# A two-layer diffusion step with experts: five PSUM banks for turning x, and four smaller edits

## The chip, the cores and the metric

One core of a Trainium2 chip runs the whole program: TensorE (matrix multiplies), VectorE (DVE), ScalarE (ACT), GpSimd (POOL) and SyncE (SP, which only issues DMAs here), with a banked accumulator memory (PSUM, eight banks of 512 fp32 columns per partition) and on-chip memory (SBUF). The metric is the device time of one execution in microseconds, as the median of three runs.

## The reference, cut to what matters

Two layers act on 384 rows of 1024 values: 128 context rows and 256 latent rows, handled as three tiles of 128 rows. With `norm` an RMS norm and `sh`, `sc`, `gt` vectors computed from a conditioning vector, one layer is

```
h = rms_norm(x, norm_g[l, 0]) * (1 + sc_m) + sh_m
y = token_mixer(h)                                # 8 attention heads, gated MLP heads, a short convolution
x = x + gt_m * rms_norm(y, norm_g[l, 1])
h = rms_norm(x, norm_g[l, 2]) * (1 + sc_f) + sh_f
f = swiglu(h) if l == 0 else moe_swiglu(h)        # (silu(h @ Wg) * (h @ Wu)) @ Wd, width 2816
x = x + gt_f * rms_norm(f, norm_g[l, 3])
```

`moe_swiglu` takes logits `h @ w_router` (1024 x 8), picks the two best experts of each row, and adds their SwiGLU outputs weighted by a softmax over the two logits. All weights are fp32 and are read once from memory.

## The kernel before, in words

Every product of full precision is three matmuls in the fast `fp32r` type: a value is split in a rounded part (`whi`, `xhi`, `hhi`) and a rest (`wlo`, `xlo`, `hlo`), and `three` (L1285) issues hi x hi, hi x lo, lo x hi. Weights come as 1 MB chunks in the order of one list (`stream`, L64) through a ring of six buffers `raw`: SP may load chunk n when TensorE has finished chunk n-6 (L433). ACT rounds each chunk to `whi` (`split`, L622 to L628), which waits for TensorE to be done with the chunk three before, and DVE makes `wlo` (L890). `upto(n)` on either engine means that all chunks up to n are split.

Each engine has one hand-written instruction order, joined to the others by semaphores. Around each of the four sub-layers the order is the following, with s = 0 to 3 counting (layer 0 mixer, layer 0 FFN, layer 1 mixer, layer 1 router).

The end of a sub-layer is `residual`. TensorE finishes y of tiles 0, 1 and 2 in PSUM banks 0 to 5. For each tile ACT squares and sums y (`rms`, L638) and takes the square root (L640); DVE takes the reciprocal (L901), multiplies (L973) and adds to x (L975). Shortly before, TensorE spreads the gate row over the partitions and ACT copies it (`gates`, L688). ACT's functions lie in tables that are loaded when a function outside the current table comes up; Exp, Silu, Gelu and Sqrt need different ones, Copy, Square and Identity none of their own. 

The next sub-layer begins with `norm`. ACT sums the squares of the new x (L638, L640), and DVE scales each tile of x into `f` (`scaled`, L948). TensorE turns x: for each of the eight k-tiles of 128 columns, three transposes (`turn_x`, L1354) bring the k-tile of the three row tiles into one PSUM bank. For s >= 1 the banks are 6 and 7 in turn (`turn_banks`, L358), and the turn of k-tile kt waits until the one of kt-2 has been read (L1380). ACT scales and shifts it into `hf` (L662 for the context rows, L663 for the latent rows), and for s < 3 DVE makes `xhi` (L955) and `xlo` (L957). The mixer's first products wait k-tile by k-tile (L1526). The dense FFN of layer 0 waits for all eight (L1752), then `gate_up` (L1649) runs over b = 0 to 10 column blocks, two chunks each; block b writes banks 0, 2, 4 or 1, 3, 5.

For s = 3, the router, TensorE puts after each turn the logits of the k-tile two before (`logits`, L1344: 24 small fp32 matmuls), and ACT alone writes `hf`. DVE then picks the experts (L1218 on), TensorE turns `hf` back to rows (L1760), counts rows per expert (L1767, L1771), and POOL scatters the rows (L583) and gathers those of each expert (L592). The experts follow, 33 chunks each, with as many row tiles as they were given (1, 1.5, 2 or 3).

At the very end POOL gathers for each row tile t the two expert outputs, `yg[:, 0, t]` and `yg[:, 1, t]` (L612), both on semaphore `s_yg[t]`. DVE multiplies the first by its gate (L1274) and adds the second times its gate (L1275), for all three tiles; then comes `residual(3, 1, 1)`, and ACT stores x (L879).

## Time and profile before

| what | value |
|---|---|
| three runs | 1779.31, 1783.63 and 1784.79 us, median 1783.63 |
| the profiled execution | 1779.33 us, of which its span is 1777.6 |
| mean granted TensorE clock | 0.963 of full |
| busy: TensorE matmul, DVE, ACT, POOL | 93%, 61%, 52%, 10% |
| DMA | 422 MB, mean 237 GB/s |

Times of the trace count from the span's start. Four stretches lie between sub-layers and are named in what follows: the first from 233 to 263 us (mixer to dense FFN), the second from 538 to 573 us (dense FFN to the second mixer), the third from 761 to 826 us (second mixer through the router to the experts), and the last from 1742 us on. A row of the timeline gives the start and duration in us, engine, line, operation and operands; `xN` merges N alike, and brackets give the idle time before it and what ended it. PEclk is the granted share of TensorE's full clock of 2.4 GHz; it has two levels, 1.0 and 0.5.

### The profile page before, as it was taken

The page shows a single profiled execution, that of the slowest core. Times are in us where ns is not written, and L with a number is a line of the kernel's source. Part 1 is how long each engine was busy: PE and PEld are TensorE (multiplying, and loading weights), DVE is VectorE, ACT ScalarE, POOL GpSimd, SP SyncE. Part 2 cuts the span into 40 slices and gives each one's busy share as a digit, 9 for nine tenths or more (in the row PEclk, how much of TensorE's full clock was granted, in tenths as well). Part 3 has the DMA queues.
Part 4 walks back from the last instruction along what each step waited for, and adds up shares of the span by engine and source line. Part 5 has one row for each costly group of instructions (what it writes and reads, how often), then busy time and mean ns, then how long its engine had stood idle before and what let it go on. Part 6 is the DMA issues. An engine that isn't in the chain of part 4 may idle for free.

```text
span 1777.6 us, 21764 instructions
## 1 busy us (share of the span) xinstructions
PE 1650.7 (93%) x8658; PEld 1293.1 (73%) x8658; DVE 1089.5 (61%) x1204; ACT 926.5 (52%) x1137; POOL 170.9 (10%) x178
## 2 busy tenths in 40 slices
PE   5799979999998899975999999999999999999993
PEld 2567758888776567754887877878787777787782
DVE  2336563333235326644998989898988866657653
ACT  1425452323225325453777777777777755455541
POOL 2400000000003000002021020303030100010001
PEclk9999979999998999986999999999999999999996
DMA  9973223333465872315999999999999976676643
GB/s 334 342 263 143 90 72 110 127 119 119 166 234 153 294 261 84 99 63 169 358 369 350 378 350 376 349 381 350 370 358 358 357 217 209 213 228 211 202 155 120
DMA packets 295809, 422.11 MB, mean 237 GB/s; under 512 B 21792, under 2 KB 226592, under 8 KB 295584
## 3 DMA queue, kind: packets, MB, share of 16 engines
q1 hardware_dynamic: 281504, 394.85, 65.7%
q0 software_dynamic: 13056, 23.11, 4.3%
q10 hardware_dynamic: 1136, 2.64, 0.4%
q8 instruction: 73, 1.20, 0.3%
q14 instruction: 40, 0.33, 0.1%
HBM read 418.56 MB, written 19.27 MB: 246 GB/s over the span
## 4 chain that ended last, share of the span: by engine, by line
PE 85%; DMA 4%; DVE 4%; ACT 2%; issue 2%; SPq 1%; POOL 1%; POOLq 0%; DVEq 0%; ACTq 0%
PE ps L1287 23%; PE ps L1289 22%; PE ps L1288 22%; PE ps L1293 3%; PE ps L1294 3%; DMA raw<-in_w_in_dram 2%; PE ps L1643 2%; PE ps L1329 1%; PE ps L1721 1%; SPq L436 1%; PE ps L1354 1%; DMA raw<-in_w_ada_dram 1%; PE ps L1477 1%; PE ps L1461 1%; PE ps L1311 1%
## 5 line engine op out<-in xcount | busy, mean ns | idle before, releaser
L890 DVE TENSOR_TENSOR wlo<-raw,whi 128x2048 fp32r<-128x2048 f32 x327 | 747.3, 2291 | 327.4 <-ACT whi L628 324.7
L628 ACT ACTIVATE whi<-raw 128x2048 fp32r<-128x2048 f32 x327 | 625.9, 1917 | 341.4 <-DMA raw<-in_w_in_dram 108.7
L1287 PE MATMUL ps<-whi,xhi 128*128 128x512 f32 (+1 forms) x1352 | 546.3, 404 | 18.2 <-DVE wlo L890 11.0
L1289 PE MATMUL ps<-whi,xlo 128*128 128x512 f32 (+1 forms) x1352 | 528.3, 391 | 0.0
L1288 PE MATMUL ps<-wlo,xhi 128*128 128x512 f32 (+1 forms) x1352 | 527.7, 390 | 0.0
L1287 PEld LDWEIGHTS ps<-whi,xhi 128*128 128x128 f32 x1352 | 258.2, 191 | 86.8 <-DVE wlo L890 25.2
L1289 PEld LDWEIGHTS ps<-whi,xlo 128*128 128x128 f32 x1352 | 257.6, 191 | 54.2
L1288 PEld LDWEIGHTS ps<-wlo,xhi 128*128 128x128 f32 x1352 | 258.5, 191 | 47.7 <-issue 0.5
L1287 PE MATMUL ps<-whi,hhi 128*128 128x512 f32 x484 | 196.3, 405 | 0.4 <-DVE pg L1007 0.4
L1289 PE MATMUL ps<-whi,hlo 128*128 128x512 f32 x484 | 189.5, 391 | 0.0
L1288 PE MATMUL ps<-wlo,hhi 128*128 128x512 f32 x484 | 189.1, 391 | 0.0
L1289 PEld LDWEIGHTS ps<-whi,hlo 128*128 128x128 f32 x484 | 90.9, 188 | 19.6
L1287 PEld LDWEIGHTS ps<-whi,hhi 128*128 128x128 f32 x484 | 91.0, 188 | 19.0 <-DVE pg L1007 1.2
L1288 PEld LDWEIGHTS ps<-wlo,hhi 128*128 128x128 f32 x484 | 91.2, 188 | 17.0 <-issue 0.2
L592 POOL DMA_INDIRECT hx<-h_rows,lidx x24 | 49.7, 2073 | 522.1 <-PE ps L1721 430.8
L718 ACT ACTIVATE pg<-ps 128x256 f32<-128x256 f32 x121 | 43.5, 380 | 97.2 <-PE ps L1643 88.2
L1005 DVE TENSOR_TENSOR pg<-pg,ps 128x256 f32<-128x256 f32 x121 | 48.6, 417 | 71.0 <-ACT pg L718 60.3
L731 ACT ACTIVATE xhi<-ps 128x384 fp32r<-128x384 f32 x64 | 31.5, 492 | 85.4 <-PE ps L1721 84.8
L605 POOL DMA_INDIRECT y_rows<-f,lidx x24 | 44.0, 1832 | 326.0 <-ACT f L757 319.3
L1329 PE MATMUL ps<-raw,cS 128*32 128x512 f32 x384 | 53.5, 675 | 21.9 <-DMA raw<-in_w_ada_dram 21.9
L1293 PE MATMUL ps<-whi,xhi 128*128 128x512 f32 x176 | 68.6, 390 | 1.8 <-DVE xhi L1026 1.8
L1294 PE MATMUL ps<-wlo,xhi 128*128 128x512 f32 x176 | 68.6, 390 | 0.0
(219 smaller groups left out, 1287.8 us busy)
## 6 DMA issues: line engine op xcount, KB each, us to landing
raw<-in_w_moe_gu_dram SPq DMA_DIRECT2D x352, 512.0 KB, 6.5
raw<-in_w_moe_d_dram SPq DMA_DIRECT2D x176, 512.0 KB, 6.3
raw<-in_w_ada_dram SPq DMA_DIRECT2D x96, 512.0 KB, 10.0
raw<-in_w_in_dram SPq DMA_DIRECT2D x44, 512.0 KB, 7.5
raw<-in_w_ffn_gu_dram SPq DMA_DIRECT2D x44, 512.0 KB, 4.6
raw<-in_w_ffn_d_dram SPq DMA_DIRECT2D x22, 512.0 KB, 6.9
raw<-in_w_out_dram SPq DMA_DIRECT2D x16, 512.0 KB, 4.4
bias<-rpb_rows POOLq DMA_DIRECT2D x32, 96.0 KB, 4.3
```

The source lines that it names most:

```text
L592: pool.indirect_dma_start(out=hx[:, i, :], out_offset=None, in_=h_rows[:, :], in_offset=bass.IndirectOffsetOnAxis(ap=lidx[:, e, i:i + 1], ...
L605: pool.indirect_dma_start(out=y_rows[:, :], out_offset=bass.IndirectOffsetOnAxis(ap=lidx[:, e, i:i + 1], axis=0), in_=f[:, i, :], in_offse ...
L628: act.activation(whi[m % SPL][:, :], raw[n % RING][:, :], ACT.Copy).then_inc(s_hi, 1)
L718: ins = act.activation(pg[:, t, :], ps[:, 2 * t + b % 2, 0:256], ACT.Silu)
L890: dve.tensor_tensor(wlo[n % RING][:, :], raw[n % RING][:, :], whi[NTH[n] % SPL][:, :].bitcast(F32), ALU.subtract).then_inc(s_lo, 1)
L1005: ins = dve.tensor_tensor(pg[:, t, :], pg[:, t, :], ps[:, 2 * t + b % 2, 256:512], ALU.mult)
L1287: pe.matmul(out, a_hi, w_hi, start=start, stop=False)
L1288: pe.matmul(out, a_hi, w_lo, start=False, stop=False)
L1289: return pe.matmul(out, a_lo, w_hi, start=False, stop=stop)
L1293: pe.matmul(out, a, w_hi, start=start, stop=False)
L1294: return pe.matmul(out, a, w_lo, start=False, stop=stop)
L1329: ins = pe.matmul(ps[32 * k:32 * k + 32, bank, :], cS[:, 4 * h + k, :], w[:, k, :], start=(h == 0), stop=(h == 1))
```

## The change

1. `turn_banks`: five banks in turn in place of two for s >= 1, and turn kt waits for the reader of kt-5 in place of kt-2.
2. For the dense FFN, the wait for all of `xlo` before `dense()` goes; in block 0, row tile 0, TensorE waits for each k-tile's `xlo` ahead of its products. It still issues the eight turns first.
3. The router: ACT writes `hf` for the even k-tiles, DVE for the odd ones (semaphore `s_hfd`), and all logits come after all turns.
4. `fetch_roots`: a square root of one column on ACT before each `gates`, and once after the experts.
5. The last combination: ACT multiplies the first choice by its gate (`first_choice`), DVE adds the second, and DVE's residual of tile t-1 comes between the combinations of t and t+1. Each gather has its own semaphore.

```diff
         def turn_banks(s):
-            return [6, 7] * (KT // 2) if s else list(range(KT))
+            if s == 0:
+                return list(range(KT))
+            free = [1, 3, 5, 6, 7] if s == 1 else [3, 4, 5, 6, 7]
+            return (free + free)[0:KT]
+
+        def rows_out(eng, kt):
+            eng.wait_ge(s_hfd if kt % 2 else s_hf, KT * 3 + kt // 2 + 1 if kt % 2 == 0 else kt // 2 + 1)
...
-                for kt in range(KT):
+                for kt in range(0, KT, 2 if s == 3 else 1):
                     act.wait_ge(s_tr, KT * s + kt + 1)
...
                 for t in range(NT):
                     if s == 3:
+                        if t + 1 < NT:
+                            first_choice(t + 1)
                         act.wait_ge(s_yc, t + 1)
...
+            def fetch_roots():
+                act.activation(root[:, :], eps[:, :], ACT.Sqrt)
+
+            def first_choice(t):
+                act.wait_ge(s_yg[0][t], 16)
+                act.activation(yg[:, 0, t, :], yg[:, 0, t, :], ACT.Copy, scale=gates_of[:, 0, t:t + 1]
+                               ).then_inc(s_ya, 1)
...
                 upto(n - 1)
+                fetch_roots()
                 gates(2 * l)
...
                     upto(PLACE["ffn", 0, N_FFN - 1])
+                    fetch_roots()
                     gates(1)
...
             by_tiles(act, "act", T, expert)
+            fetch_roots()
+            first_choice(0)
             residual(3, 1, 1)
...
                 if s:
                     scaled(s, l, half)
-                for kt in range(KT if s < 3 else 0):
+                if s == 3:
+                    dve.wait_ge(s_modc, 2 * l + half + 1)
+                    for kt in range(1, KT, 2):
+                        dve.wait_ge(s_tr, KT * s + kt + 1)
+                        sh, sc = modc[:, 2 * half, kt, :], modc[:, 2 * half + 1, kt, :]
+                        for g, a, b in ((0, 0, P), (1, P, 3 * P)):
+                            ins = dve.tensor_scalar(hf[:, kt, a:b], ps[:, turn_banks(s)[kt], a:b], sc[:, g:g + 1],
+                                                    sh[:, g:g + 1], ALU.mult, ALU.add)
+                        ins.then_inc(s_hfd, 1)
+                    return
+                for kt in range(KT):
...
             for t in range(NT):
-                dve.wait_ge(s_yg[t], 32)
-                chain(dve.tensor_scalar(yg[:, 0, t, :], yg[:, 0, t, :], gates[:, 0, t:t + 1], None, ALU.mult))
+                dve.wait_ge(s_yg[1][t], 16)
+                dve.wait_ge(s_ya, t + 1)
                 dve.scalar_tensor_tensor(out=yg[:, 0, t, :], in0=yg[:, 1, t, :], scalar=gates[:, 1, t:t + 1],
                                          in1=yg[:, 0, t, :], op0=ALU.mult, op1=ALU.add).then_inc(s_yc, 1)
-            residual(3, 1, 1)
+                if t:
+                    residual(3, 1, 1, [t - 1])
+            residual(3, 1, 1, [NT - 1])
...
             def norm(s):
                 for kt in range(KT):
-                    if kt == 1 and s % 2 == 0:
+                    if kt == 1 and s == 2:
                         pe.wait_ge(s_modc, s + 1)
-                    if kt >= 2:
-                        pe.wait_ge(s_hf, KT * s + kt - 1)
+                    if kt >= 5:
+                        if s == 3:
+                            rows_out(pe, kt - 5)
+                        else:
+                            pe.wait_ge(s_hf, KT * s + kt - 4)
                     turn_x(s, kt)
-                    if s == 3 and kt >= 2:
-                        if kt == 2:
-                            pe.wait_ge(s_wr, 16)
-                        logits(kt - 2)
                 if s == 3:
-                    for kt in (KT - 2, KT - 1):
-                        pe.wait_ge(s_hf, KT * s + kt + 1)
+                    pe.wait_ge(s_wr, 16)
+                    for kt in range(KT):
+                        rows_out(pe, kt)
                         logits(kt)
...
                             for kk in range(4):
                                 kt = 4 * h + kk
+                                if ready is not None and b == 0 and t == 0:
+                                    ready(kt)
...
-                gate_up(NT, 0, n0)
+                def ready(kt):
+                    pe.wait_ge(s_xlo, KT + kt + 1)
+
+                gate_up(NT, 0, n0, ready=ready)
...
                 norm(2 * l + 1)
                 if l == 0:
-                    pe.wait_ge(s_xlo, KT * 2)
                     dense()
```

## Rows read from the trace of the kernel before

**Rows 1.** The page, chain that ended last: shares of the span by engine
```profile
PE 85%; DMA 4%; DVE 4%; ACT 2%; issue 2%; SPq 1%; POOL 1%; POOLq 0%; DVEq 0%; ACTq 0%
```

**Rows 2.** Windows (us, each engine's busy time, PEclk, DMA share, GB/s): an expert
```profile
931.00:1030.00 99.00, 99.00 (x448) 78.85 (x447) 87.97 (x75) 74.95 (x76) 14.73 (x8) 1.00 1.06 363
```

**Rows 3.** Timeline, first stretch: ACT and DVE around the first square root
```profile
234.45 0.60 ACT L688 ACTIVATE f<-ps 128x512 f32<-128x512 f32 x1 [6.68 <-PE ps L1624]
...
239.56 2.29 DVE L890 TENSOR_TENSOR wlo<-raw,whi 128x2048 fp32r<-128x2048 f32 x1 [9.46 <-ACT whi L628]
...
241.08 1.28 ACT L640 ACT_TABLE_LOAD   x1
...
242.71 0.16 DVE L901 RECIPROCAL rs<-rs 128x1 f32<-128x1 f32 x1 [0.85 <-ACT rs L640]
```

**Rows 4.** Timelines of PE, ACT and DVE, first stretch: the turns of x
```profile
253.39 1.12 PE L1354 MATMUL ps<-ident,f 128*128 128x128 f32 x4 [0.39 <-DVE f L948]
...
263.20 0.80 PE L1287 MATMUL ps<-whi,xhi 128*128 128x512 f32 x1 [2.74 <-DVE xlo L957]
...
253.97 0.46 ACT L662 ACTIVATE hf<-ps,modc 128x128 f32<-128x128 f32 x1 [1.70 <-PE ps L1354]
...
254.77 0.46 ACT L662 ACTIVATE hf<-ps,modc 128x128 f32<-128x128 f32 x1
...
254.91 0.36 DVE L955 CAST xhi<-hf 128x384 fp32r<-128x384 f32 x1 [1.58 <-ACT hf L663]
...
255.78 0.35 DVE L955 CAST xhi<-hf 128x384 fp32r<-128x384 f32 x1
...
260.63 1.05 DVE L955 CAST xhi<-hf 128x384 fp32r<-128x384 f32 x1
```

**Rows 5.** Timelines of DVE and PE, second stretch
```profile
552.33 2.29 DVE L890 TENSOR_TENSOR wlo<-raw,whi 128x2048 fp32r<-128x2048 f32 x1 [5.49 <-ACT whi L628]
555.80 0.16 DVE L901 RECIPROCAL rs<-rs 128x1 f32<-128x1 f32 x1 [1.17 <-ACT rs L640]
...
566.48 1.11 PE L1354 MATMUL ps<-ident,f 128*128 128x128 f32 x4 [0.39 <-DVE f L948]
...
573.19 0.78 PE L1287 MATMUL ps<-whi,xhi 128*128 128x512 f32 x1
...
575.90 0.43 PE L1287 MATMUL ps<-whi,xhi 128*128 128x512 f32 x1
```

**Rows 6.** Timelines of PE and DVE, third stretch: turns and logits
```profile
781.18 1.12 PE L1354 MATMUL ps<-ident,f 128*128 128x128 f32 x4 [0.38 <-DVE f L948]
...
783.55 0.51 PE L1344 MATMUL ps<-wr,hf 128*32 128x8 f32 x24
...
789.92 0.83 PE L1344 MATMUL ps<-wr,hf 128*32 128x8 f32 x48
...
791.57 0.18 DVE L1218 COPY lg<-ps 128x24 f32<-128x24 f32 x1 [10.45 <-PE ps L1344]
```

**Rows 7.** Instructions of tile f: DVE's scaling of 256 columns from PSUM
```profile
L1083 DVE TENSOR_SCALAR f<-ps x16: 414/414/416, 159.1 to 722.0; 128x256 f32<-128x256 f32 x16
```

**Rows 8.** Windows of 2 us: the clock's rise, first and third stretch
```profile
268.00:270.00 2.00, 2.00 (x9) 1.61 (x8) 0.00 (x0) 0.00 (x0) 0.00 (x0) 0.81 0.00 0
...
794.00:796.00 2.00, 1.85 (x14) 1.40 (x13) 0.53 (x5) 1.44 (x4) 0.00 (x0) 0.89 0.00 0
```

**Rows 9.** Timeline of the last stretch, DVE
```profile
1758.37 0.75 DVE L1274 TENSOR_SCALAR yg<-yg,gates 128x1024 f32<-128x1024 f32 x1 [13.36 <-DMA yg<-y_rows,idx]
...
1761.83 0.75 DVE L1274 TENSOR_SCALAR yg<-yg,gates 128x1024 f32<-128x1024 f32 x1 [1.39 <-DMA yg<-y_rows,idx]
...
1764.49 0.75 DVE L1274 TENSOR_SCALAR yg<-yg,gates 128x1024 f32<-128x1024 f32 x1 [0.58 <-DMA yg<-y_rows,idx]
...
1773.29 1.23 DVE L975 TENSOR_TENSOR x<-x,yg 128x1024 f32<-128x1024 f32 x1
```

**Rows 10.** Instructions of tile yg: the six gathers from issue to landing
```profile
DMA to landing us min/median/max: 4.5/5.8/6.3
```

More of the change, by code:

```diff
@@ L958, in norm, with residual @@
                                       ).then_inc(s_xlo, 1)
-            def residual(s, l, half):
+            def residual(s, l, half, tiles=range(NT)):
                 r = 5 * l + 2 + 2 * half
-                for t in range(NT):
+                for t in tiles:
                     g = min(t, 1)
@@ L1647, in turn, with gate_up @@
                     ins.then_inc(s_ht, 1)
[L1649 removed]
+            def gate_up(T, k, n0, free=None, half=0, ready=None):
                 for b in range(GU_B):
```

9 lines of the change are left out of this document (6 added, 3 removed).

## The prediction

> **What bounds the kernel.** I read the page first. Part 4 puts 85% of the chain that ended last on TensorE [rows 1], so the kernel is a long stream of matmuls, and time can only be won where TensorE stands still or runs slow. The waits of TensorE and the merged chain then say where: at the four stretches between sub-layers. I read those instruction by instruction in the timelines of each engine, and the clock in windows of 2 us. The experts I read in one window each: TensorE is busy all the time at full clock, and the DMA engines are as full, at 363 GB/s [rows 2]. So nothing is to be won inside the experts. What starts them earlier counts in full only if the weight stream starts earlier too. It does: SP loads a chunk when TensorE has finished the one six before, so with the ring full the stream waits for TensorE. Before the experts the DMA share is 0.00 [rows 8].
>
> **The square root table (edit 4).** In the first stretch ACT ends its squares and loads a table for 1.28 us; only then come the root and DVE's reciprocal at 242.71 [rows 3]. The early load falls in the 6.68 us in which ACT waits for the gates' matmul [rows 3], so it costs nothing; without that cover it would cost its 1.28 us in front of the gates, which is no more than it saves. What is late next is DVE: its `wlo` ends at 239.56 + 2.29 = 241.85, so the reciprocal comes at about 241.8, 0.9 us earlier and not 1.28. From there DVE works in one chain through three tiles and three scalings, so x reaches TensorE 0.9 us earlier. In the second stretch `wlo` ends at 554.62 and the reciprocal stood at 555.80 [rows 5]: 1.15 us. The third has the first's pattern: 0.9 us. In the last the load is off the path already.
>
> The Trainium skill, "ScalarE: Activation LUTs", section "What ACT_TABLE_LOAD costs", counts about 2.66 us for a switch, of which some 1.38 is a drain. Here the root follows the load directly and the load is 1.28, so the measurement decides. By the page each of the three loads would hide twice as much, but DVE's `wlo` would cap the gain at the values above all the same, or at most 1.4 us more each if the drain lay on this path.
>
> **First stretch: five banks and the FFN by k-tile (edits 1, 2).** The last transposes of k-tile 0 begin at 253.39. Four take 1.12 us of which one's own length is 0.47, so they start 0.215 us apart, 0.65 us per k-tile [rows 4]. ACT needs 254.77 - 253.97 = 0.80 us for a k-tile, DVE 255.78 - 254.91 = 0.87 us [rows 4]. With two banks the three engines took turns, and TensorE then waited 2.74 us for the last `xlo`, until 263.20.
>
> After: with the 0.9 us, k-tile 0's last transpose starts at 252.5. Counting it, 22 transposes remain, 22 x 0.215 = 4.7 us, if the bank is free each time. K-tile 5 is due at 252.5 + 13 x 0.215 = 255.3 and needs ACT's k-tile 0 (about 254.0), k-tile 7 is due at 256.6 and needs ACT's k-tile 2 (about 255.6). So no wait: the turns end at about 257.3. The FFN's chunks 0 and 1 are split before the residual. Its first product needs `xlo` of k-tile 0, ready at 255.78 - 0.9 = 254.9, and k-tile 3 is ready at about 257.6, or 258.3 if the slow cast of 1.05 us [rows 4] falls on it. At the low clock a k-tile's three matmuls take 1.3 us, so TensorE asks for k-tile 3 at 261.2. K-tiles 4 to 7, ready by 262, are asked for after 12 k-tile products, past 270. The eight new waits therefore cost nothing, and the products start at 257.3 and not at 263.2: 5.9 us, the table's 0.9 within it. The bounds: 2 us if the turns run only at ACT's pace, or if xlo starves the products; 6.5 us if nothing waits.
>
> **The clock.** In this stretch the granted clock is at 0.5 until about 268.8 (0.81 over 268 to 270 is 0.76 us at the low level) [rows 8], 5.6 us after the first product. In the second it comes back at about 575.9, 2.7 us after the first product at 573.19: before it six matmuls take 2.71 us, 0.45 each, against about 0.22 in an expert [rows 5, 2]. In the second there was no gap between turns and products, and so it will be in both now. If the first goes from 5.6 to 2.7 us at half speed it gains 1.4; if the second goes the other way it loses 1.4. I take 0.6 for the first, near the middle, and 0 for the second. For both together the ends are -1.4 and +2.8.
>
> **Second stretch (edit 1).** K-tile 0's last transpose moves from 566.48 to 565.33, and 22 x 0.215 later, at 570.1, the first product can start, in place of 573.19 [rows 5]. It already waited k-tile by k-tile; `xlo` 0 is ready at about 567.8, k-tile 3 at about 570.8 while TensorE asks for it at 574. Gain 3.1 us, the table's 1.15 within it. POOL's DMAs fall in the same time and DVE's casts are slower in places; at the low end 1.5 us.
>
> **Third stretch (edits 1, 3).** TensorE was nearly the bound of the router: from 781.18 to the logits' copy at 791.57, with a turn and a logits group in 1.27 us [rows 6]. The last two groups ran together in 0.83 us with 0.20 for one's length, or 0.32 a group; in alternation one cost 0.44. After: start 780.3, turns until 785.0 as above, then 0.3 us to switch, 8 x 0.32 = 2.6 us and 0.2 for the last, so the copy comes at 788.2: 3.4 us, of which 0.9 the table's. DVE's new pair costs 0.41 for 256 columns [rows 7] and by that row some 0.28 for 128, 0.6 to 0.7 in all; it does four, ACT four at 0.80. Both keep up with 1.3 us of turns per pair. K-tile 7 is written by 786.1, and its logits are asked for at 787.5. If the logits keep 0.44 a group the gain is 2.4. Behind it the clock stays at 0.5 until 794.2 [rows 8], inside the turning back of hf. If it still rises at that hour, what then stands in front at the low clock costs about 0.5 us more; if it doesn't rise before the counting matmuls, about 3. I take 3.0 us, bounds 0.4 and 3.6. Scatters, gathers and experts hang on this chain and shift whole.
>
> **Last stretch (edit 5).** DVE's third combination waits for its gather (0.58 us idle), the end of x is 1773.29 + 1.23 = 1774.52 [rows 9]. From the second pair's landing at 1761.8 DVE now has two combinations of 1.31 and three residuals of 2.65 (reciprocal, 1.28, 1.23 and the gaps): 10.6 us, to 1772.4. ACT must keep up. The gathers land 4.5 to 6.3 us after issue [rows 10], and tile 1's first choice about halfway between 1758.3 and 1761.8 [rows 9], so ACT has it scaled at 1761.2, does tile 0's squares and root until 1762.7, before DVE asks at 1763.1; then scales tile 2 until 1764.2, and tile 1's root is ready at 1765.7 while DVE asks at 1766.9. The new wait in front of `rms` on ACT has tile 0's squares behind it and costs nothing here. If tile 1's first choice lands only with its second, DVE is 1.1 us later. Gain 2.1, bounds 0.8 and 2.3.
>
> **Sum.** 5.9 + 0.6 + 3.1 + 3.0 + 2.1 = 14.7 us. Against the profiled execution, 1779.33, that is 1764.6. The median before is 1783.63, 4.3 above it, for which the trace has no reason, so I set the sum against the median: 1768.9.
>
> **The rivals.**
> - The gain is partly eaten: turns go at ACT's pace or the first products starve, and the router's matmuls stay in the low clock. Then 2 + 1.5 + 0.4 + 2.1 and little from the clock, with some of these at their better end: about 8 us, 1775.6. For it: at 0.65 against 0.80 us per k-tile ACT is the slower engine, and DVE slower still. Against it: five banks' slack covers eight k-tiles.
> - Edit 4 does not do what it says, the tables being loaded again at the roots: 0.9 + 1.15 + 0.9 less, 11.8 us, 1771.8. Against it: copies after a root in this trace bring no load.
> - The weight stream takes it back: the experts' DMA is full at 363 GB/s [rows 2]. If it, and not TensorE's start, set the end, only the last stretch would count: 1781.5. Against it: a share of 0.00 before the experts [rows 8].
> - Slower than before: the clock. Without the idle gap TensorE goes from turns to products at 0.5, and if it is not granted full speed for long afterwards, each us at the low level costs half a us. From 29 us more at 0.5 the gain is gone, and 40 us more in both blocks together gives 1789. For it: the level does fall in every stretch. Against it: it rose within 2.7 to 5.6 us of the first product in the two stretches.
>
> **Chances.** The forecast, with its own range 1764 to 1774, 0.60; table again 0.05; partly eaten 0.22; stream 0.08; clock 0.03; the remaining 0.02 is more than the sum. What this measurement can tell from no change is 0.3%, 5.4 us. From the cases: faster 0.88, same 0.09, slower 0.03. The range is 1762 to 1777, with the spread of the three runs, up to 4 us below and 1 above the median, in it.
>
> **What will show it.** No ACT_TABLE_LOAD between the first squares and their root in the three stretches; reciprocals directly behind `wlo`. The first FFN product 4 to 5 us after the last scaling of x, straight behind the 24th transpose. The lg copy about 8 us after k-tile 0's last transpose. DVE without a gap from the second landing to the end. It would be wrong if the first products show waits for xlo, if an expert takes longer than before, or if the low clock lasts over 10 us into a sub-layer.

## The result, and the profile after

| what | before | after |
|---|---|---|
| median, and the runs behind it | 1781.99 us, 4 runs (1779.31 to 1784.79) | 1760.11 us, 4 runs (1759.11 to 1761.90) |
| ratio of the two | | 0.9878, 95% interval 0.9859 to 0.9898 |
| profiled execution, its span | 1779.33, 1777.6 | 1759.84, 1758.1 |
| mean granted clock | 0.963 | 0.969 |

The kernel became faster by 1.2%: 21.9 us by the medians, 19.5 us between the two profiled executions. The forecast was 1768.9 with a range of 1762 to 1777. The direction was right, the size was 8.8 us short, and the time lies below the range.

To see where the 19.5 us came from, I cut both spans at the same eleven instructions. A stage here runs from the instruction in its first column to the next one's.

```
stage, from ... to ...                                      before   after    diff
start, to the gates' matmuls of the first stretch           233.40  234.03   +0.63
first stretch, to the first FFN product                      29.80   23.66   -6.14
dense FFN, to the gates' matmuls of the second stretch      275.19  273.16   -2.03
second stretch, to the mixer's first product                 34.80   31.54   -3.26
second mixer, to the gates' matmuls of the third            188.00  186.58   -1.42
third stretch, to DVE's copy of the logits                   30.38   24.74   -5.64
picking, scatter and gather, to the first gathered turn      26.01   25.37   -0.64
to the experts' first product                                 9.02    9.02    0
experts, to the last gates' matmul                          919.52  921.08   +1.56
last stretch, to the end of x                                28.40   25.85   -2.55
to the end of the span                                        3.08    3.07    0
```

The first, fifth and ninth lines carry the spread from one execution to the next. Over the sixteen profiled executions behind this document the start takes 230.2 to 236.6 us. The experts take 919.3 to 922.1 (925.8 in one) and the second mixer 185.7 to 190.9. Where the code of the stage is the same as in the kernel after, the first stretch takes 23.0 to 23.7 us, the FFN 272.6 to 273.2, the second stretch 30.6 to 31.6, and the last stretch 25.7 to 26.6. The third took 24.74 us where the low clock (below) lasted 6.8 us, and 26.14 in e7, where it lasted 10.2.

The page of the kernel after: part 1 and the chain that ended last by engine, to be set beside [rows 1]. TensorE's share of the chain fell from 85% to 81%.

```profile
PE 1637.8 (93%) x8658; PEld 1288.4 (73%) x8658; DVE 1090.2 (62%) x1209; ACT 924.9 (53%) x1136; POOL 172.6 (10%) x178
...
PE 81%; DMA 7%; DVE 6%; ACT 2%; issue 2%; SPq 1%; POOL 1%; POOLq 0%; DVEq 0%; ACTq 0%
```

Timelines of ACT, DVE and PE of the kernel after, first stretch, which answer to [rows 3, 4]:

```profile
241.49 0.19 ACT L649 ACTIVATION_READ_ACCUMULATOR hf<-ps 128x1 f32 x1
241.71 0.29 ACT L651 ACTIVATE rs<-ss,eps 128x1 f32<-128x1 f32 x1
...
240.19 2.29 DVE L917 TENSOR_TENSOR wlo<-raw,whi 128x2048 fp32r<-128x2048 f32 x1 [9.47 <-ACT whi L639]
242.40 0.16 DVE L928 RECIPROCAL rs<-rs 128x1 f32<-128x1 f32 x1
...
253.08 4.96 PE L1393 MATMUL ps<-ident,f 128*128 128x128 f32 x22 [0.39 <-DVE f L975]
257.69 0.78 PE L1326 MATMUL ps<-whi,xhi 128*128 128x512 f32 x1
258.69 0.40 PE L1328 MATMUL ps<-whi,xlo 128*128 128x512 f32 x1
...
258.06 1.21 DVE L992 CAST xhi<-hf 128x384 fp32r<-128x384 f32 x1
```

No table load stands between the squares and the root, and the reciprocal follows `wlo` at once. All 22 remaining transposes form one row of 4.96 us, where four stood in a row before. The product comes directly behind them, without a bracket and so without a wait. The durations of the products show the clock, which came back to full speed at 258.7: the first takes 0.78 us, the third 0.40.

The second stretch of the kernel after, timelines of DVE and PE (compare [rows 5]):

```profile
544.77 2.29 DVE L917 TENSOR_TENSOR wlo<-raw,whi 128x2048 fp32r<-128x2048 f32 x1 [5.47 <-ACT whi L639]
546.98 0.15 DVE L928 RECIPROCAL rs<-rs 128x1 f32<-128x1 f32 x1
...
557.78 4.89 PE L1393 MATMUL ps<-ident,f 128*128 128x128 f32 x22 [0.39 <-DVE f L975]
562.39 0.52 PE L1326 MATMUL ps<-whi,xhi 128*128 128x512 f32 x1
```

And the third (compare [rows 6]). The turns and the logits are now two rows, and the second turning follows:

```profile
768.02 3.91 PE L1393 MATMUL ps<-ident,f 128*128 128x128 f32 x22 [0.39 <-DVE f L975]
771.86 1.79 PE L1383 MATMUL ps<-wr,hf 128*32 128x8 f32 x192
773.58 1.09 PE L1803 MATMUL ps<-ident,hf 128*128 128x128 f32 x8
...
769.24 0.86 DVE L986 TENSOR_SCALAR hf<-ps,modc 128x128 f32<-128x128 f32 x2 [1.28 <-PE ps L1393]
773.71 0.18 DVE L1255 COPY lg<-ps 128x24 f32<-128x24 f32 x1 [0.76 <-PE ps L1383]
```

The same 22 transposes take 3.91 us here and about 4.9 in the first two stretches. The reason stands in the windows of 2 us (columns as in [rows 2]: PEclk is third from the right). Of the kernel after:

```profile
258.00:260.00 2.00, 2.00 (x9) 1.59 (x8) 1.97 (x4) 2.00 (x6) 1.60 (x3) 0.83 0.00 0
562.00:564.00 2.00, 2.00 (x11) 1.74 (x10) 1.94 (x4) 2.00 (x7) 2.00 (x4) 0.88 0.56 146
770.00:772.00 2.00, 2.00 (x30) 1.83 (x33) 1.65 (x5) 1.74 (x5) 0.00 (x0) 0.83 0.00 0
```

A PEclk of 0.83 over 2 us is 0.68 us at the low level (1.2 GHz in place of 2.4) and the rest at full. Narrower windows give the edges. The low periods about the three stretches were 20.5, 13.6 and 17.1 us long before and are 10.2, 6.8 and 6.8 us after. Before, the clock came back 5.6 us behind the first FFN product, 2.8 behind the mixer's, and 2.8 behind the logits' copy [rows 8]. After, it comes back 1.0 us behind the first FFN product, at the mixer's first product, and at 770.7, two thirds through the router's turns.

The last stretch, DVE of the kernel after (compare [rows 9]), with ACT's new multiply:

```profile
1742.49 1.15 ACT L704 ACTIVATE yg<-yg,gates 128x1024 f32<-128x1024 f32 x1 [2.06 <-DMA yg<-y_rows,idx]
...
1744.59 1.28 DVE L1312 SCALAR_TENSOR_TENSOR yg<-yg,gates 128x1024 f32<-128x1024 f32 x1 [2.06 <-DMA yg<-y_rows,idx]
...
1753.80 1.23 DVE L1012 TENSOR_TENSOR x<-x,yg 128x1024 f32<-128x1024 f32 x1
```

From 1744.59, when the second pair of rows has landed, to 1755.03 DVE never waits.

### The profile page after: what moved, and what is told of

Its sections match the earlier page's. It is cut to its first block, busy times and chain, and to the rows that moved or that the text cites. A ratio compares the mean times of both kernels' runs of the same rounds, so it can differ in the third digit from the quotient of the medians.

```text
span 1758.1 us, 21774 instructions
## 1 busy us (share of the span) xinstructions
PE 1637.8 (93%) x8658; PEld 1288.4 (73%) x8658; DVE 1090.2 (62%) x1209; ACT 924.9 (53%) x1136; POOL 172.6 (10%) x178
## 4 chain that ended last, share of the span: by engine, by line
PE 81%; DMA 7%; DVE 6%; ACT 2%; issue 2%; SPq 1%; POOL 1%; POOLq 0%; DVEq 0%; ACTq 0%
PE ps L1326 22%; PE ps L1328 21%; PE ps L1327 21%; DMA raw<-in_w_in_dram 3%; PE ps L1332 3%; PE ps L1333 3%; DMA raw<-in_w_moe_gu_dram 2%; DVE wlo L917 2%; PE ps L1682 2%; ACT whi L639 2%; PE ps L1368 1%; PE ps L1765 1%; SPq L447 1%; PE ps L1393 1%; PE ps L1516 1%
```

## The experiments

All are the changed kernel with one edit, except b1 and e9, which start from the kernel before. Medians are "this / the kernel before in the same set", with the ratio's 95% interval. The kernel after stands at 0.9878 [0.9859, 0.9898]. A kernel's own runs in one set lie 3 to 11 us apart, so effects of 1 to 3 us are read from the stages. The stages of each profiled execution, cut as above ("first" is the first stretch, "end" the last stretch to the end of x):

```
        start  first    FFN second  mixer  third gather  experts   end
b1     233.23  29.80 275.34  34.81 189.69  30.38  26.21   920.89 28.32
after  234.03  23.66 273.16  31.54 186.58  24.74  25.37   921.08 25.85
e1     233.54  24.61 272.87  32.08 186.31  26.65  25.36   920.09 25.98
e2     230.60  25.77 273.96  33.66 190.90  25.36  25.39   919.34 25.91
e3     235.02  28.21 274.41  30.57 185.91  26.07  25.39   920.20 25.95
e4     232.93  23.35 272.67  31.19 186.29  26.67  25.43   922.10 26.18
e5     235.24  23.67 273.14  31.55 186.54  24.75  25.38   919.27 28.40
e6     230.94  22.85 272.84  30.84 185.96  26.33  26.88   925.79 26.57
e7     233.35  23.30 272.60  31.18 186.36  26.14  35.21   919.80 26.11
e8     230.18  22.82 272.71  30.89 186.24  26.36  35.69   920.75 25.97
e9     233.82  29.42 275.48  31.76 186.01  30.39  26.32   919.41 28.47
e10    231.95  22.85 272.82  30.85 189.74  28.17  26.84   920.92 26.09
e11    235.63  23.01 272.70  30.98 186.33  29.40  26.94   920.17 25.66
e12    235.61  22.84 272.84  30.84 185.68  24.77  28.44   919.50 25.93
e13    236.59  23.67 273.05  31.56 186.41  27.37  26.46   921.75 25.94
```

### The parts, one undone at a time

**e1: the square roots' tables are no longer fetched early.**

```diff
-                fetch_roots()
                 gates(2 * l)
...
-                    fetch_roots()
                     gates(1)
```

> The changed kernel without the early square roots (edit 4 undone). My theory: the table load comes back between tile 0's squares and its root in three stretches, and DVE's wlo had hidden part of it, so the reciprocals stand 0.85 us behind wlo in the first and third stretch and 1.2 us in the second: about 2.9 us slower than the changed kernel, near 1763. The rival, the Trainium skill's page ScalarE: Activation LUTs, counts a drain on top, which would make each stretch up to 1.4 us worse still, about 7 us in all.

Measured 1764.53 / 1783.44, 0.9898 [0.9874, 0.9922]. ACT's and DVE's timelines of e1, first stretch and then second:

```profile
241.23 1.28 ACT L651 ACT_TABLE_LOAD   x1
...
242.85 0.16 DVE L926 RECIPROCAL rs<-rs 128x1 f32<-128x1 f32 x1 [0.85 <-ACT rs L651]
...
548.43 0.16 DVE L926 RECIPROCAL rs<-rs 128x1 f32<-128x1 f32 x1 [1.17 <-ACT rs L651]
```

The load is back with its 1.28 us, and DVE waits 0.85 and 1.17 us for it, as in the kernel before. The first stretch is 0.95 us longer, the second 0.54 and the third 1.91. In the third the low clock lasted 10.2 us in place of 6.8, so the turns ran slower as well (4.88 us in place of 3.91). By e7 that also happens without this edit, and against e7, with the same low clock, the third stretch is 0.51 longer. So the table costs 2.0 to 3.4 us in all, where 2.9 had been expected. The other rival's 7 us, with a drain on top of each load, is refuted too: the root follows its load at once, and DVE's wait is no longer than the load explains. The prediction's rival by which the tables would be loaded again is refuted: the load vanishes with the edit and returns without it.

**e2: two banks in turn for the first two stretches.**

```diff
-            free = [1, 3, 5, 6, 7] if s == 1 else [3, 4, 5, 6, 7]
+            if s < 3:
+                return [6, 7] * (KT // 2)
+            free = [3, 4, 5, 6, 7]
...
+                    if s < 3 and kt >= 2:
+                        pe.wait_ge(s_hf, KT * s + kt - 1)
```

> The changed kernel with banks 6 and 7 in turn again for s = 1 and 2 (edit 1 undone there), the products of the dense FFN still by k-tile. My theory, formed on the changed kernel's trace: it is the gapless run of 22 transposes that brings the granted clock back to 1.0 at the first product. With two banks the turns take 6.8 us from k-tile 0's last transpose in place of 4.6, in both stretches, 4.4 us in all, and the clock comes back about 2.7 us after the first product and not with it, 1.3 us more in each: 7 us slower than the changed kernel, 1767. The rival, that the clock's return is chance and has nothing to do with the banks: 4.4 us, 1764.5, and the low level ends within 1 us of the first product.

Measured 1766.17 / 1783.44, 0.9904 [0.9882, 0.9926]. First stretch, timeline of PE, then the windows of both stretches, of e2:

```profile
255.01 1.71 PE L1395 MATMUL ps<-ident,f 128*128 128x128 f32 x6 [0.20 <-ACT hf L676]
256.37 0.78 PE L1328 MATMUL ps<-whi,xhi 128*128 128x512 f32 x1
...
258.00:260.00 2.00, 2.00 (x8) 1.54 (x7) 1.93 (x6) 1.47 (x1) 1.01 (x2) 0.73 0.02 4
566.00:568.00 2.00, 2.00 (x10) 1.60 (x9) 0.99 (x3) 0.00 (x0) 2.00 (x5) 0.93 0.47 166
```

TensorE waits for ACT in each turn again, and the product comes 2.11 and 2.12 us later in its stretch. The clock comes back 2.7 and 2.3 us behind the products, after 13.6 us at the low level in both. With five banks those were 1.0 and 0 us, after 10.2 and 6.8. The dense FFN is 0.80 us longer. The mixer is 4.3 longer, but 2.3 us of low clock at its head explain 1.2 of that at most, and this stage also took 189.7 in b1 and e10. The three executions with two banks took 188.0 to 190.9 there, and twelve of the thirteen with five 185.7 to 186.6; what more than the clock lies behind it stays open.

One execution could be chance, but over all sixteen the time from k-tile 0's last transpose to the clock's next return is 9.0 to 15.4 us in the six runs of turns with two banks (the first two stretches of before, b1 and e2) and 2.5 to 5.6 in the 26 with five banks, nowhere between. So the clock's early return comes with the gapless turns: seen in both stretches, and worth 0.8 us in the FFN.

**e3: the dense FFN waits again for all of `xlo`, behind five-bank turns.**

```diff
                 if l == 0:
+                    pe.wait_ge(s_xlo, KT * 2)
                     dense()
...
-                gate_up(NT, 0, n0, ready=ready)
+                gate_up(NT, 0, n0)
```

> The changed kernel with the dense FFN waiting for all of xlo again (edit 2 undone), five banks kept. My theory: the first product comes when DVE ends k-tile 7's xlo, 4.8 us later than now, and since the turns had brought the clock back already, the FFN runs at full clock from its first product: 4.8 us slower, 1764.9. The rival, that the products and not the turns bring the clock back: a low level for 3 to 5.6 us after the first product, 1.5 to 2.8 us more, 1767.

Measured 1765.37 / 1783.44, 0.9892 [0.9870, 0.9914]. Timeline and windows of PE in e3:

```profile
254.08 3.82 PE L1393 MATMUL ps<-ident,f 128*128 128x128 f32 x22 [0.39 <-DVE f L975]
263.23 0.79 PE L1326 MATMUL ps<-whi,xhi 128*128 128x512 f32 x1 [5.33 <-DVE xlo L994]
...
256.00:258.00 2.00, 1.90 (x15) 1.66 (x13) 1.93 (x5) 2.00 (x6) 0.03 (x1) 0.85 0.00 0
260.00:262.00 2.00, 0.00 (x0) 0.00 (x0) 1.91 (x5) 2.00 (x4) 0.22 (x1) 0.50 0.02 4
266.00:268.00 2.00, 2.00 (x9) 1.58 (x8) 0.00 (x0) 0.00 (x0) 0.00 (x0) 0.79 0.00 0
```

The clock came back in the turns, at 256.6. In the wait of 5.33 us it fell again, and it returned only 3.6 us behind the product. My expectation that it would stay up was wrong. The price is 4.55 us in the stretch and 1.25 in the FFN.

**e9: the kernel before with five banks alone, for the first two stretches.**

```diff
-            return [6, 7] * (KT // 2) if s else list(range(KT))
+            if s == 0:
+                return list(range(KT))
+            if s == 3:
+                return [6, 7] * (KT // 2)
+            free = [1, 3, 5, 6, 7] if s == 1 else [3, 4, 5, 6, 7]
+            return (free + free)[0:KT]
...
-                    if kt >= 2:
+                    if s == 3 and kt >= 2:
                         pe.wait_ge(s_hf, KT * s + kt - 1)
+                    if s < 3 and kt >= 5:
+                        pe.wait_ge(s_hf, KT * s + kt - 4)
```

> The kernel before with five banks for s = 1 and 2 (edit 1 alone, without the router). My theory: in the first stretch DVE's xlo of k-tile 7 still ends the wait, so the first product comes only 0.6 us earlier; in the second the turns end 2.1 us earlier and the products follow. With the clock's earlier return (2.7 and 1.3 us sooner against the first product) about 2 us more: 4 to 5 us faster than the kernel before, near 1777. The rival, five banks are worth their slots everywhere: 2.1 us in both stretches before any clock, 6 to 7 us, 1775.

Measured 1776.50 / 1781.49, 0.9973 [0.9954, 0.9992]. PE's timeline of e9, first stretch:

```profile
253.82 4.96 PE L1359 MATMUL ps<-ident,f 128*128 128x128 f32 x22 [0.38 <-DVE f L953]
...
263.24 0.79 PE L1292 MATMUL ps<-whi,xhi 128*128 128x512 f32 x1 [4.47 <-DVE xlo L962]
```

The turns are gapless, yet the product stands where it did: TensorE waits 4.47 us for the last `xlo` in place of 2.74 [rows 4]. In that wait the clock, back since 258.9, falls again, and returns 5.9 us behind the product, so the FFN gains nothing (275.48 us). Five banks are worth 0.38 us in the first stretch and 3.05 in the second. In e2 the FFN by k-tile and the table were worth 4.03 in the first without the banks. Together the three edits bring 6.14 (of which e1 gives the table 0.95). In the second stretch, where the products already waited k-tile by k-tile, the banks bring nearly all.

**e4: ACT alone writes `hf` in the router, logits still after the turns.**

```diff
-            eng.wait_ge(s_hfd if kt % 2 else s_hf, KT * 3 + kt // 2 + 1 if kt % 2 == 0 else kt // 2 + 1)
+            eng.wait_ge(s_hf, KT * 3 + kt + 1)
...
-                for kt in range(0, KT, 2 if s == 3 else 1):
+                for kt in range(KT):
...
-                    for kt in range(1, KT, 2):
+                    for kt in range(0):
```

> The changed kernel with all eight hf k-tiles of the router written by ACT (half of edit 3 undone), five banks and logits after all turns kept. My theory: ACT needs 0.80 us per k-tile and now sets the end: hf of k-tile 7 is written 6.5 us after ACT's first, the copy of the logits comes 1.8 us later than in the changed kernel: 1761.9. The rival, that TensorE's turns and logits are the bound and the split is worth nothing: no difference, 1760.1.

Measured 1758.45 / 1783.44, 0.9853 [0.9830, 0.9876]. PE and DVE of e4:

```profile
772.65 0.38 PE L1382 MATMUL ps<-wr,hf 128*32 128x8 f32 x24 [0.33 <-ACT hf L674]
773.10 0.18 DVE L1254 COPY lg<-ps 128x24 f32<-128x24 f32 x1 [7.68 <-PE ps L1382]
```

The last logits wait for ACT. The third stretch is 26.67 us, 1.93 longer than the changed kernel's, but the low clock lasted 10.2 us here. Against e7, with the same clock and both engines, it is 0.53 longer. So DVE's share of the copies is worth 0.5 us for sure; the 1.8 that I had expected looked confirmed until e7 was there to compare. The total is no longer than the changed kernel's.

**e11: logits between the turns again, banks and two engines kept.**

```diff
+                    if s == 3 and kt >= 2:
+                        rows_out(pe, kt - 2)
                     turn_x(s, kt)
+                    if s == 3 and kt >= 2:
+                        if kt == 2:
+                            pe.wait_ge(s_wr, 16)
+                        logits(kt - 2)
                 if s == 3:
-                    pe.wait_ge(s_wr, 16)
-                    for kt in range(KT):
+                    for kt in (KT - 2, KT - 1):
```

> The changed kernel with the router's logits back between the turns (k-tile kt-2 after turn kt), five banks and two copying engines kept. My theory: alternation costs TensorE 0.12 us a k-tile and thins out the run of turns, so the clock returns about 3.4 us later in the router, and the transposes and counts behind run longer at the low level: the logits' copy comes 2 us later than now and the gather 0.5 us more, 2.5 us slower, 1762.6. The rival, that copying on two engines alone made the router faster: no difference, 1760.1.

Measured 1764.13 / 1781.49, 0.9906 [0.9883, 0.9930]. PE's timeline of e11, third stretch:

```profile
770.07 0.51 PE L1383 MATMUL ps<-wr,hf 128*32 128x8 f32 x24
770.52 0.90 PE L1393 MATMUL ps<-ident,f 128*128 128x128 f32 x3
...
777.91 5.58 PE L1808 MATMUL ps<-ident,hf 128*128 128x128 f32 x24
```

The third stretch is 29.40 us, 4.66 longer, and 1.57 more are lost behind it; I had expected 2.5. From 769.24 to 777.27 turns and logits follow one another without a wait, but at the low level, which lasts from 763.1 to 783.6: 20.5 us in place of 6.8. It ends 0.1 us behind the 24 transposes that turn `hf` back, which stand in one row again. So the absence of waits alone did not bring the clock back here. Against the 30.38 of before, the 0.98 left is what the early table gives, so two engines and five banks in the old order are worth nothing. The order of the logits is the router's gain, and the clock comes with it: 13.7 us more at the low level, over TensorE's work and its gaps. The four executions with the old order (before, b1, e9, e11) had 17.1 to 20.5 us at the low level here. Without extra work ahead of these turns, the ten with the new order had 6.8 or 10.2.

**e5: the old combination at the end.**

```diff
-            first_choice(0)
             residual(3, 1, 1)
...
-                dve.wait_ge(s_ya, t + 1)
+                chain(dve.tensor_scalar(yg[:, 0, t, :], yg[:, 0, t, :], gates[:, 0, t:t + 1], None, ALU.mult))
...
-                if t:
-                    residual(3, 1, 1, [t - 1])
-            residual(3, 1, 1, [NT - 1])
+            residual(3, 1, 1)
```

> The changed kernel with the old last combination (edit 5 undone; the early root after the experts stays). My theory: from the gates' matmul at the end to the last x the stretch takes the 28.4 us of the kernel before again in place of 25.9: 2.5 us slower, 1762.6. The rival, that the early root and not the reordering shortened this stretch: no difference, 25.9.

Measured 1760.18 / 1780.41, 0.9885 [0.9862, 0.9908]. The last stretch is 28.40 us, that of the kernel before to the hundredth, against 25.85: 2.55 us, expected 2.5. The other executions with the new end took 25.66 to 26.57, so it is 1.8 to 2.7. The early root is still there in e5, so it was not the root that shortened this stretch. The median does not show it; two kernels within 3 us of each other can't be told apart by four runs.

**b1: the kernel before, once more.**

> The kernel before, unchanged, in a second profiled execution. My theory: most of the 2.0 and 1.4 us that the sub-layers behind the first and second stretch gained is the clock's earlier return, and the hour of that return has chance in it also with the same instructions: the low level, 20.5 us long in the first stretch and 13.6 in the second, will differ by some us, and with it the product stages, by less than 1 us each; stretches up to the first product repeat within 0.3 us (29.8 and 34.8 us). The rival, that the clock's return is fixed by the instructions: the same lengths.

Measured 1782.50 in one run. The first three stretches repeat within 0.01 us, and the low clock lasted 20.5 and 13.6 us in the first two, as before. So I was wrong that it would differ by some us there. In the third it lasted 20.5 instead of 17.1, with the same 30.38 us to the logits' copy. These stages can be compared between single executions; the mixer (+1.69) and the experts (+1.37) can't.

### Can the low clock be avoided altogether?

TensorE is idle for about 5.5 us before the turns. If it has work there, does the clock stay up? `keep_busy(n)` issues n extra fp32 matmuls of 512 columns into bank 6, whose result nobody reads.

```diff
+            def keep_busy(n):
+                for i in range(n):
+                    pe.matmul(ps[:, 6, :], selb[:, 0, :], gate_f[:, 0:512], start=True, stop=True)
...
             def norm(s):
+                pe.wait_ge(s_gtc, 4 * s)
+                keep_busy(5)                       # e6, e8: every s but 0; e10: not s = 3
...
             T = tiles_of(pe)
+            keep_busy(18)                          # e7, e8; e10: 6
```

**e6: before the turns of all three stretches.**

> The changed kernel with five extra matmul calls (fp32, 512 columns, into bank 6, results unused; about 4.4 us at full clock) ahead of the turns of x in the three stretches, where TensorE stands still for 5.5 us. My theory: the clock is a term of its own, and with TensorE busy it stays at 1.0 through turns and first products. The turns then go as fast as ACT and DVE let them; the first row tile's products of the FFN end 2 us earlier, those of the mixer 1.3 us, the logits come 1.4 us earlier: 4.7 us faster than the changed kernel, 1755.4. The rival, that what the changed kernel's clock won is chance: the low level stays as it is in the three stretches, and nothing is gained or lost, 1760.1.

Measured 1758.58 / 1780.41, 0.9875 [0.9858, 0.9891]. PE's timeline and windows of e6, first stretch:

```profile
242.65 4.45 PE L1418 MATMUL ps<-gate_f,selb 128*128 128x512 f32 x10
248.27 0.33 PE L1394 MATMUL ps<-ident,f 128*128 128x128 f32 x1 [1.16 <-DVE f L976]
249.99 4.05 PE L1394 MATMUL ps<-ident,f 128*128 128x128 f32 x22 [0.53 <-DVE f L976]
...
248.00:250.00 2.00, 0.67 (x3) 0.29 (x3) 1.86 (x5) 0.83 (x3) 0.00 (x0) 0.89 0.00 0
252.00:254.00 2.00, 2.00 (x15) 2.00 (x14) 1.93 (x5) 2.00 (x6) 0.00 (x0) 0.76 0.00 0
```

In the first two stretches the clock did not stay up. It still fell, at 249.5 in the first, just before the long run of turns, and came back 3.4 us later. In the third it did stay up, through all turns and up to the standstill shown next. The four stages behind the extra work gain 0.81, 0.32, 0.70 and 0.62 us. Then the router loses 1.59 and the stage behind it 1.51, where PE's timeline of e6 shows something new:

```profile
765.16 1.66 PE L1384 MATMUL ps<-wr,hf 128*32 128x8 f32 x176
769.29 0.40 PE L1384 MATMUL ps<-wr,hf 128*32 128x8 f32 x16 [2.48 <-issue]
```

TensorE stands 2.48 us inside the logits, with nothing shown that it waits for, and the low clock follows (768.4 to 775.2). I had expected 4.7 us from this kernel; it gained nothing that can be measured. e8, with the same matmuls ahead, stands 2.51 us at the same place.

**e7 and e8: in the wait for the gathered rows; e8 with e6's as well.**

> The changed kernel with 18 such extra matmul calls (some 15.7 us at full clock) where TensorE waits 18.8 us for the experts' first gather. My theory: now the clock is at 0.5 from 781 to 811.7, through the turns of the gathered rows and 3.5 us into the first expert; with TensorE busy it stays at 1.0, the products win 1.7 us and the turns 1 to 2: 3 us faster, 1757. If the experts' stream of weights at 360 GB/s set their end and not TensorE's start, these 3 us would be lost again by the last gates' matmul.

> Both sets of extra matmuls, those ahead of the turns and those in the wait for the gather. My theory: the gains add, 7.7 us less than the changed kernel, 1752.4, and the granted clock's mean rises from 0.969 to about 0.99. The rival, chance: 1760.1.

Measured 1767.03 / 1780.41, 0.9927 [0.9910, 0.9943], and 1765.12 / 1780.41, 0.9914 [0.9894, 0.9934]. PE's timeline of e7:

```profile
765.84 4.95 PE L1394 MATMUL ps<-ident,f 128*128 128x128 f32 x22 [0.39 <-DVE f L976]
...
789.66 18.64 PE L1418 MATMUL ps<-gate_f,selb 128*128 128x512 f32 x36 [10.16 <-issue]
```

Up to 777 us e7 is the changed kernel. Yet its 22 turns took 4.95 us in the third stretch, not 3.91, as the clock came back only at 771.7: 1.40 us by chance alone. The extra matmuls start 10.16 us late. For the first 2.6 of these TensorE's next instruction waits for the tile counts, which DVE writes at 782.1; the other 7.6 pass where the kernel loads these counts into TensorE's registers. So they run past the rows' arrival: the gathered turn comes 9.84 us later (10.32 in e8). The clock at the head of the experts returns 1.64 us, far less. I had put the work in the wrong place in time, and the attempt was a loss.

**e10: five before the first two turns only, six behind the register loads.**

> The changed kernel with the five extra matmul calls only ahead of the turns of s = 1 and 2, none in the router, and six in the wait for the gather, which end before the gathered rows land. By the stages of the two runs before: 0.8 + 0.3 + 0.7 + 0.6 us from the two sub-layers and 1.6 us from the gathered rows' turns, 4 us faster than the changed kernel, 1756.1. The rival, that the experts' full weight stream takes the last part back: 2.4 us, 1757.7.

Measured 1760.89 / 1781.49, 0.9876 [0.9856, 0.9896], where I had expected 1756.1. The gains of e6 repeat (0.81, 0.34, 0.69), but the third stretch is 3.43 us longer, although nothing was added in it; chance by e7 is 1.4 of that at most. The six calls in the gap win 0.88 us at the head of the experts, where I had expected 1.6. PE's timeline of e10:

```profile
772.14 1.97 PE L1384 MATMUL ps<-wr,hf 128*32 128x8 f32 x186
776.08 0.24 PE L1384 MATMUL ps<-wr,hf 128*32 128x8 f32 x6 [1.97 <-issue]
```

The standstill stays, but ten positions later: 176 logits before it with 30 extra instructions ahead (a matmul of this type is two), 186 with 20. So I asked whether it sits at a fixed place in TensorE's sequence of instructions. With 12 extra it should then come after 194, which is 2 past the last logit.

**e12: three calls before the first two turns. e13: five calls of 8 columns in place of 512.**

> The changed kernel with three extra matmul calls (12 instructions of 0.43 us in all, two per call) ahead of the turns of s = 1 and 2, none elsewhere. My theory on the stall of 2 to 2.5 us in the router's logits, seen with 30 extra instructions after 176 of the 192 and with 20 extra after 186: it sits at a fixed place of TensorE's instruction sequence, so with 12 extra it falls after some 194, just behind the logits, and the router's stage up to the logits' copy is 24.7 us again. The low level in the first two stretches is shorter, the stages of the two sub-layers win about 1.5 us together: 1758.6. The rival, that the busy stretches before it bring the stall on: a stall among the logits again, 28 us for that stage.

> The changed kernel with 20 extra instructions of 8 columns (five calls ahead of the turns of s = 1 and of s = 2), which keep TensorE busy for well under 1 us. My theory, a fixed place in the instruction sequence: the stall comes after 186 logits' matmuls, as with 20 long ones. The rival, the busy time: no stall, 24.7 us to the logits' copy. What it takes off or adds elsewhere is nothing in both.

e12 measured 1762.12 / 1782.15, 0.9899 [0.9879, 0.9918], where I had expected 1758.6; e13 1760.55 (two runs) / 1782.15, 0.9882 [0.9840, 0.9924]. PE's timelines of e12, behind its 192 logits, and of e13:

```profile
772.45 0.44 PE L1812 MATMUL ps<-ident,hf 128*128 128x128 f32 x2
774.83 0.88 PE L1812 MATMUL ps<-ident,hf 128*128 128x128 f32 x6 [1.95 <-issue]
```

```profile
774.25 1.74 PE L1384 MATMUL ps<-wr,hf 128*32 128x8 f32 x186
778.35 0.24 PE L1384 MATMUL ps<-wr,hf 128*32 128x8 f32 x6 [2.36 <-issue]
```

Both came as the fixed place says: after 192 + 2, and after 186 with tiny matmuls too. So the place depends on how many instructions stand ahead, not on how long they take. The rival of e12, that busy stretches bring the standstill on, is refuted by e13. In e12 the third stretch is clean (24.77 us), and the loss is paid behind it, 3.07 us. The changed kernel's own place would be 206, 14 transposes into the turning back. No standstill is visible there, where TensorE has waits of its own.

The trace holds a candidate. Besides the kernel's own transfers it records DMAs of a kind named instruction, and one of them runs at each standstill. From `--dma` of e6, 766.5 to 768.5 us, its only transfer in these 2 us:

```profile
q8 instruction: 1, 0.02, 3.0%
```

It is the 35th load of this queue in all five executions, 16 KB each. In e6 it runs from 766.97 to 767.92, and TensorE goes on at 769.29. In e8, e10, e12 and e13 as well it starts between 0.7 us before the standstill and 0.2 behind its beginning, and TensorE goes on 1.3 to 1.5 us behind its end. That fits a TensorE that runs through 192 very short matmuls faster than its instructions arrive, and a place that is counted in instructions. In the kernel after, the same load runs from 773.50 to 774.45, and TensorE doesn't stand still for it, so it needs more than the load. No run here moves the load by itself: the cause is likely but not shown.

None of these kernels beat the changed one by more than the spread.

## Why the forecast was wrong

**The start and the bounds: right.** TensorE's standing and slow stretches were where the time was. The weight stream took nothing back: the experts need 921.08 us after 919.52, and 919.3 to 922.1 in nearly all kernels with the same code there.

**The table, the turns, the FFN by k-tile: right in mechanism and size.** First stretch 6.14 us against 5.9, second 3.26 against 3.1. The 22 transposes took 4.96 and 4.89 us against 4.7, the reciprocal followed `wlo` at once, and no product waited for `xlo`, even with a cast of 1.21 us in the way. What I had not seen is that the two edits of the first stretch need each other: five banks alone only move the wait (0.38 us, e9).

**The last stretch: right.** 2.55 us against 2.1. DVE's chain from the second landing took 10.44 us against 10.6.

**The failed step is "The clock", and with it the size of the third stretch.** I took 0.6 us for the first stretch and 0 for the second: the clock would come back 2.7 us behind the first product in both, because the second stretch "had no gap between turns and products, and so it will be in both now". That compared the wrong gap. The turns themselves had gaps, waits for a bank, and e2 shows what they did: with two banks the return is indeed 2.7 and 2.3 us behind the product, as I had forecast for the change. With gapless turns it is 1.0 and 0. The FFN thus has 5.6 - 1.0 = 4.6 us less at half speed, or 2.3 us of time, and 2.03 were measured. The mixer has 2.7 us less, 1.35 of time; 1.42 were measured, in a stage that varies by more. Together 3.45 us against 0.6, and above my upper end of 2.8. In e4, e7 and e11, with the same code up to the FFN's products, the clock was even back ahead of the first one, and the FFN took 272.6 to 272.7 us.

**The third stretch: 3.0 us taken, 6.28 measured (5.64 to the copy and 0.64 behind it), bound 3.6.** The order of events was as forecast. The speed was not: I worked all of it at the low level, 0.215 us a transpose and 0.32 us a logits group, and kept the clock's return at its old hour. It came back at 770.7, two thirds through the turns. From k-tile 0's last transpose to the copy I had 7.9 us; it was 5.69. The turns with the switch behind them were 1.15 us shorter than forecast, and the 192 logits took 1.79 us, 0.22 a group. Behind the copy I had expected to lose about 0.5; the stage gained 0.64, with the turning back at full clock from its first instruction. Some of this is luck: with the low period of 10.2 us in e7 the gain to the copy would be 4.24, still over my bound. e11 confirms the rest: with the old order the clock stays low for 20.5 us, and 6.2 us of the change are gone. In both places the step that failed is the same: I treated the end of a low period as a date, when it moved with what TensorE did.

**The sum.** Against the profiled executions I forecast 14.7 us and 19.5 were measured: +0.2, +0.2 and +0.4 in the first, second and last stretch, +2.85 from the clock in the sub-layers, +3.3 in the third stretch, and -2.2 from the start and the experts, which the change doesn't touch. The other 4 us of the miss against 1768.9 come from the number that the sum was set against. The median of three runs stood 4.3 us above the profiled execution; with a fourth run it fell to 1781.99, and the changed kernel's median stands 0.3 from its own profiled time. But in the later sets, of 7 to 10 runs, the kernel before has medians of 1780.41 to 1783.44. So it was the profiled execution before that was a fast one, and a forecast against it would have come nearer (1764.6) only because two errors cancel. The gain itself was missed by 4.8 us between the profiled executions, and by 7.2 between the medians.

**The rivals.** "Partly eaten" is refuted: neither turns nor products waited. The table came back in none of the three stretches (e1 shows what it would have cost). The stream took nothing. The rival of a slower clock went the other way, though e3 shows its mechanism is real: a wait of 5.33 us behind the turns lets the level fall once more, for 1.25 us in the FFN.

## What to carry to other kernels

Where TensorE's clock has fallen, removing the gaps between transposes can pay twice, first by the gaps and then by an earlier return of full speed: here it came back 2.5 to 5.6 us after the start of the turns in place of 9.0 to 15.4. No gap is not enough by itself, since with logits between the turns (e11) it stayed low for 20.5 us. So after moving work, work out anew where the low period ends, and give that term bounds that reach to no low clock at all. A change that lets TensorE start sooner is only worth its gain if the next thing is ready too: five banks and the FFN by k-tile brought 0.4 and some 3 us of the first stretch by themselves, and over 5 together. Compare stages between profiled executions for effects of 1 to 3 us (and repeat even those: the clock alone moved one by 1.4). And state a forecast as a gain before it is a time: the profiled execution before stood 1.1 to 4.1 us below the later medians of the same kernel.

## What the runs showed of the hardware that I had not expected

- Low periods of the clock around the three stretches were 3.4, 6.8, 10.2, 13.6, 17.1 or 20.5 us long, over all sixteen executions. In the first two stretches they were 13.6 and 20.5 with two banks, at most 10.2 at a time with five, and 3.4 with five and extra matmuls of 512 columns until shortly before the turns. The same code gave 6.8 in one execution and 10.2 in another.
- Logits matmuls of 8 columns, four in turn into different groups of 32 partitions, follow each other every 9.3 ns at full clock (192 in 1.79 us, after).
- TensorE stood still for 1.95 to 2.51 us at a fixed place of its instruction sequence, counted in instructions: after 176, 186, 186 and 194 small matmuls with 30, 20, 20 and 12 instructions added ahead (e6 and e8, e10, e13, e12). A kernel can lose 2 us and a clock period by an edit hundreds of us earlier. A 16 KB load of instructions runs at each of these places; that it is the cause is not shown.
- In e7, 10.16 us passed between TensorE's last matmul and the extra ones behind its register loads, none of it with a releaser in the trace; by DVE's row of the tile counts 2.6 of them are a wait for DVE. The wait for the gathers hides it in the changed kernel.
